# Products with the old RWKV and retention states moved between main products; rate transposes split over three places

## The reference

```python
# layer 0: FFN, RWKV-7 || retention, FFN;  layer 1: FFN, gated DeltaNet, FFN
def ab_mixer(h, ...):
    z = h @ ab_w_in                        # one projection for both head groups
    ...
    # RWKV-7, 8 heads, state S [64, 64]:
    sk = einsum('bhvk,bhk->bhv', S, kk_t)
    S = S * w_t - sk * (kk_t * a_t)^T + v_t * k_t^T
    o = einsum('bhvk,bhk->bhv', S, r_t)
    # retention, 4 heads, state S [128, 128]:
    o = inner + (q_c @ S) * xi
    S = g_chunk * S + kz_c^T @ v_c
    out = concat([gn(o_a) * gate, gn(o_b) * silu(gr)]) @ ab_w_out
def gdn_mixer(h, ...):
    ...                                    # conv, L2 norm, chunked gated delta rule
    g = -exp(A_log) * softplus(a_in + dt_bias)     # the decay rates
    beta = sigmoid(b_in)                           # the write rates
```

## Time and profile before

| what | value |
|---|---|
| median of three runs | 1469.47 us |
| the profiled execution's own time | 1475.2 us |
| its span in the trace | 1473.4 us |
| PE busy | 1409.7 us, 96% |
| DVE, ACT, POOL busy | 61%, 44%, 31% |
| mean granted TensorE clock | 0.986 of 2.4 GHz |

### The profile page before, as it was taken

How to read it: one execution, slowest core, us unless ns; L and a number is a source line. 1 busy time by engine, 2 the same in 40 slices (tenths; PEclk the granted TensorE clock), 3 DMA queues, 4 the chain that set the end, 5 groups by cost and what they waited for, 6 DMA issues and landing times.

```text
span 1473.4 us, 30676 instructions
## 1 busy us (share of the span) xinstructions
PE 1409.7 (96%) x12120; PEld 1341.9 (91%) x12120; DVE 902.7 (61%) x1204; ACT 648.0 (44%) x983; POOL 455.2 (31%) x464
## 2 busy tenths in 40 slices
PE   7999999887999999999999999999998899999996
PEld 7999999877979799999999999998987769999996
DVE  4444456976564465654577775568777466655544
ACT  4333336534234354333453443377683345333333
POOL 3333032632324122215211127431016651211343
PEclk9999999999998999999999999999998999999999
DMA  7555543311224155555445555434334015555541
GB/s 284 170 159 185 162 152 100 103 32 31 92 87 151 65 193 159 169 165 177 147 140 159 162 176 177 142 95 143 118 120 146 31 72 186 157 159 168 181 158 52
DMA packets 50623, 203.39 MB, mean 138 GB/s; under 512 B 5697, under 2 KB 5697, under 8 KB 49761
## 3 DMA queue, kind: packets, MB, share of 16 engines
q1 hardware_dynamic: 46224, 181.03, 38.6%
q0 software_dynamic: 4016, 19.81, 3.7%
q10 hardware_dynamic: 288, 1.18, 0.2%
HBM read 192.17 MB, written 9.83 MB: 137 GB/s over the span
## 4 chain that ended last, share of the span: by engine, by line
PE 84%; DVE 8%; ACT 4%; issue 3%; POOL 1%; DMA 0%; ACTq 0%; POOLq 0%; DVEq 0%
PE gemm L2634 23%; PE gemm L2638 23%; PE gemm L2635 23%; DVE wlo L2571 2%; ACT whi L2566 2%; PE gemm L2670 1%; PE job L1763 1%; PE job L876 1%; PE job L1702 0%; PE job L551 0%; PE job L2643 0%; PE job L1670 0%; POOL xsum L3177 0%; PE job L894 0%; DVE M L2296 0%
## 5 line engine op out<-in xcount | busy, mean ns | idle before, releaser
L2634 PE MATMUL gemm<-xhi,whi 128*128 128x290 f32 (+1 forms) x2032 | 615.4, 303 | 18.2 <-DVE wlo L2571 16.2
L2571 DVE TENSOR_TENSOR wlo<-raw,whi 128x1024 fp32r<-128x1024 f32 (+1 forms) x319 | 437.5, 1372 | 305.9 <-ACT whi L2566 303.4
L2566 ACT ACTIVATE whi<-raw 128x1024 fp32r<-128x1024 f32 (+1 forms) x319 | 358.4, 1123 | 599.3 <-PE gemm L2638 595.7
L2638 PE MATMUL gemm<-xlo,whi 128*128 128x290 f32 (+1 forms) x2032 | 606.9, 299 | 1.8 <-DVE xlo L407 1.5
L2635 PE MATMUL gemm<-xhi,wlo 128*128 128x290 f32 (+1 forms) x2032 | 604.0, 297 | 0.0
L2634 PEld LDWEIGHTS gemm<-xhi,whi 128*128 128x128 f32 x2032 | 386.6, 190 | 32.4 <-DVE wlo L2571 19.0
L2638 PEld LDWEIGHTS gemm<-xlo,whi 128*128 128x128 f32 x2032 | 385.8, 190 | 3.3 <-DVE xlo L407 2.0
L2635 PEld LDWEIGHTS gemm<-xhi,wlo 128*128 128x128 f32 x2032 | 386.6, 190 | 1.7
L2634 PE MATMUL gemm<-hhi,whi 128*128 128x288 f32 x704 | 209.6, 298 | 2.6 <-POOL hlo L3193 1.9
L2635 PE MATMUL gemm<-hhi,wlo 128*128 128x288 f32 x704 | 209.6, 298 | 0.0
L2638 PE MATMUL gemm<-hlo,whi 128*128 128x288 f32 x704 | 209.2, 297 | 0.0
(11 more groups left out here) (449 smaller groups left out, 1505.6 us busy)
## 6 DMA issues: line engine op xcount, KB each, us to landing
raw<-in_w_dram SPq DMA_DIRECT2D x255, 512.0 KB, 3.5
raw<-in_w_dram SPq DMA_DIRECT2D x64, 704.0 KB, 4.1
M<-in_ret_in_dram POOLq DMA_DIRECT2D x1, 2048.0 KB, 10.6
out_ret_s_dram<-M POOLq DMA_DIRECT2D x1, 2048.0 KB, 9.2
s_space<-in_gdn_in_dram POOLq DMA_DIRECT2D x4, 512.0 KB, 5.2
M<-in_gdn_in_dram POOLq DMA_DIRECT2D x4, 512.0 KB, 5.7
out_gdn_s_dram<-s_space POOLq DMA_DIRECT2D x4, 512.0 KB, 4.2
out_gdn_s_dram<-M POOLq DMA_DIRECT2D x4, 512.0 KB, 6.7
```

The costliest lines, as they stand in the source:

```text
L2566: nc.scalar.activation(whi[c % SPL][:, 0:w], raw[c % RAW][:, 0:w], ACT.Copy).then_inc(hi_ready, 1)
L2571: nc.vector.tensor_tensor(wlo[c % SPL][:, 0:w], raw[c % RAW][:, 0:w], whi[c % SPL][:, 0:w].bitcast(F32), ALU.subtract).then_inc(lo_ready, 1)
L2634: pe.matmul(bank[:, 0:w_], whi[s][:, w], hi[:, f0 + q, 0:w_], start=first, stop=False)
L2638: mm = pe.matmul(bank[:, 0:w_], whi[s][:, w], lo[:, f0 + q, 0:w_], start=False, stop=last)
```

## The change

The old-state products are taken out of the pieces between units and called by `stage` (and by `first_half`) after each single main product, through a new argument `within`. `within_unit(k, n)` says what follows main product n of unit k of `zb`: in unit 4 the sixteen pairs of head pairs 0 and 1, in unit 5 those of head pairs 2 and 3 after the first sixteen main products and the eight sample values after the last eight, in unit 15 the sixteen retention products of heads 0 and 1 after its seventh to twenty-second main product. Heads 2 and 3 stand after the first eight main products of the two first halves of `abo`. The pieces after units 4, 14 and 15 and the work after the stage are put in a new order on PE, ACT and DVE. In the DeltaNet layer the write rates' transposes go behind unit 14 of `qk`, the decay rates' stay behind the stage, and the samples' rates' go behind unit 0 of `v`.

```diff
-            def from_state(h):
-                bank = start(("rQ", h))
-                for b in range(DB):
...
+            def from_state(h, b):
+                bank = rbanks[h]
+                mm = pe.matmul(bank[:, 4 * b:4 * b + 4], b_s0[:, h, b, :], b_qx[:, h, SEQ + 4 * b:SEQ + 4 * b + 4],
+                               start=True, stop=True)
...
+            def state_in_half(h):
+                def between(n):
+                    if n < DB:
+                        from_state(h, n)
+                rbanks[h] = start(("rQ", h))
+                return between
...
-            def old_products(ts):
...
+            def old_product(t, b):
+                o, at = (t * DB + b) * 8, SEQ + DS * b
+                mms = [pe.matmul(pbanks[e][half(e), o:o + 8], a_s0[half(e), t, b, :],
+                                 kr[half(e), t, :, at:at + DS], start=True, stop=True) for e in range(2)]
...
+            def sample_values(h, bank):
+                mm = pe.matmul(bank[NROW, h * 64:(h + 1) * 64], s_at[:, h, 64:96],
+                               a_nat[NROW, 2, 0, h * 64:(h + 1) * 64], start=True, stop=True)
...
+            def within_unit(k, n):
+                if k == 4:
+                    if n == 0:
+                        pe.wait_ge(sem("rwkv_in"), 16)
+                    if n < 16:
+                        old_product(n // DB, n % DB)
+                elif k == 5:
+                    if n < 16:
+                        old_product(2 + n // DB, n % DB)
+                    else:
+                        if n == 16:
+                            rbanks["sMV"] = start(("sMV", 0))
+                        sample_values(n - 16, rbanks["sMV"])
+                elif k == 15:
+                    if n == 6:
+                        pe.wait_ge(sem("qx"), 1)
+                        pe.wait_ge(sem("ret_in"), 16)
+                        for h in range(2):
+                            rbanks[h] = start(("rQ", h))
+                    if 6 <= n < 22:
+                        from_state((n - 6) // DB, (n - 6) % DB)
...
-            stage("zb", 1, lambda k: next(piece))
-            from_state(3)
+            stage("zb", 1, lambda k: next(piece), within=within_unit)
+            first_half("abo", 2, 0, state_in_half(2))
+            ret_out(2)
+            ret_sum("rgm", 0)
+            ret_sum("rgm", 1)
+            first_half("abo", 2, 1, state_in_half(3))
             ret_out(3)
+            ret_sum("rgv", 0)
             ret_sum("rgm", 2)
             ret_sum("rgv", 1)
-            first_half("abo", 2, 0)
...
-            ret_square(1)
-            ret_ln(0)
-            state_part(3)
             act.wait_ge(sem("y_rwkv"), 1)
             for d in range(4):
                 high_part(d, a_gate[:, d, :])
+            state_part(0)
...
+                if k == 14:
+                    bank = start(("gtokb", 0))
...
             def l2_sums(k):
+                if k == 0:
+                    sample_rates()
...
                         pe.matmul(bank[:, 0:w_], whi[s][:, w], hi[:, f0 + q, 0:w_], start=first, stop=False)
+                        if within:
+                            within(4 * i + j, 3 * q)
```

More of the change, by code:

```diff
@@ L835, in between_units @@
                     fin(mm, ("rS", j))
[L836 to L839, removed]
+                yield
                 pe.wait_ge(*out(("ratt", 1)))
@@ L1092, in ab_scalar @@
                 high_part(d, a_gate[:, d, :])
+            state_part(0)
+            state_part(1)
+            ret_copy(0)
+            ret_copy(1)
+            state_part(2)
+            ret_copy(2)
+            ret_square(0)
+            ret_square(1)
+            state_part(3)
             ret_copy(3)
+            ret_ln(0)
             ret_square(2)
@@ L1632, in decays, with write_rates @@
                 fin(pe.matmul(bank[:, 0:T], sel[R32, h, :], rows_g, start=True, stop=True), ("dgb", h))
[L1634 to L1640, removed]
+            def write_rates(k):
+                decays(k)
+                if k == 14:
+                    bank = start(("gtokb", 0))
+                    for ck in range(4):
+                        for e in range(2):
+                            mm = pe.matmul(bank[half(e), ck:16:4], rows_b[:, ch_of(ck)], C("ident")[0:8, e:8:2],
+                                           start=True, stop=True)
+                    fin(mm, ("gtokb", 0))
+            stage("qk", 5, write_rates)
             bank = start(("gtok", 0))
@@ L1647, in gdn_tensor, with sample_rates @@
             fin(mm, ("gtok", 0))
[L1648 to L1656, removed]
+            def sample_rates():
+                pe.wait_ge(sem("rows4"), 3)
+                for key, ns, rows in ((("gtok4b", 0), (0,), slice(0, HC)), (("gtok4", 0), (1, 2), R32)):
+                    bank = start(key)
+                    for n in ns:
+                        for g in range(2):
+                            at = 2 * (n - ns[0]) + g
+                            mm = pe.matmul(bank[:, at:at + 1], q_rows[n][:, hs(g), :], C("ones", rows)[:, 0:1],
+                                           start=True, stop=True)
+                    fin(mm, key)
             def l2_sums(k):
+                if k == 0:
+                    sample_rates()
                 for t in (2 * k - 2, 2 * k - 1):
@@ L2164, in gdn_vector, with from_rows @@
                      key)
[L2165 to L2168, removed]
+            def from_rows(k):
+                if k == 1:
+                    for key, n0, n in ((("gtok4b", 0), 0, 1), (("gtok4", 0), 1, 2)):
+                        dve.wait_ge(*full(key))
+                        read(V.tensor_copy(q_tok[:, n0:n0 + n, :], jb(key, 2 * n).rearrange("p (n g) -> p n g", n=n)),
+                             key)
+                l2_max(k)
+            env["stage"]("v", conv(16, from_rows))
             l2_max(8)
```

77 lines of the change are left out of this document (31 added, 46 removed).

## The result

| | before | after |
|---|---|---|
| median of four runs each, one chip | 1469.16 us (1467.29 to 1469.93) | 1497.16 us (1493.71 to 1498.37) |
| ratio | | 1.0189, 95% interval 1.0172 to 1.0205 |
| profiled execution | 1475.2 us | 1493.71 us |

A forecast was written before the change was run, and what follows sets the result against it. PE, busy 96% of the span, and its clock were taken to bound the kernel. Units 4 to 6 +26.7, retention -2.3 and rates -0.8 sum to +23.6 us, giving 1493 on the 1469.5 median, range 1473 to 1502.

The forecast's parts named there:

- PE and its clock bound these stages: PE busy 96% of the span, so its instructions and clock are nearly the whole time.
- An insertion with change of form: Units 4 and 5: a singly placed pair adds 0.45 us, making 0.58 per main product; 0.96 at half clock.
- The clock falls in the middle of unit 4 and stays low into unit 6: Clock falls half way through unit 4's sixteen insertions, until main products follow each other again in unit 6.
- Units 4 to 6: RWKV's insertions: unit 4 +8.9, between units -2.5, unit 5 +17.3, unit 6 and its small groups +3.0; sum +26.7 us.
- Retention -2.3: Unit 15 and first halves of `abo`: one of two low-clock stretches gone, -3.3; new wait +1.0; range -6.7 to +4.
- The wait on ACT: Before the first half of `abo`, PE waits for ACT to drain head 0's job bank: +1.0 us, between 0 and 1.4.
- Rates -0.8: Rates' transposes in three places: two more changes of form +0.8 us, clock expected to hold -1.6 us.
- Rival 1: Clock holds in units 4 and 5 because PE never idles: +6.9 us, so 1476; chance 0.15.
- rivals 2 and 3: Weight loads hidden even where the form changes, about 1461, chance 0.09; loads half hidden, no change, 1467 to 1472, chance 0.04.
- Rival 4: As forecast, but the clock also stays low through retention's 32 insertions: 1499 us; chance 0.07.

The follow-up runs named there:

- RWKV's part alone: Only RWKV's old-state products and sample values moved as in the changed kernel, retention and rates left as before the change: 1490.59 us, ratio 1.0144.
- groups of eight: Changed kernel with RWKV's pairs in four groups of eight and the sample values as one group: 1476.54 us, ratio 1.0056; second run 1484.77 us.
- kernel with 128x128 forms: Changed kernel with each pair of 64x64 products made one product with 128x128 weights and the same 8 columns: 1490.48 us, ratio 1.0134.

## Why the prediction was right, and where not

The forecast was 1493 (range 1473 to 1502), the measured median 1497.16. The mechanism held where most of the time lies, in units 4 to 6; that the sum came so near is in part luck (see the base). Point by point:

- **PE and its clock bound these stages.** Right: PE's busy time grew with the span.
- **An insertion with change of form.** The term was 0.45 us and a period 0.58 at full clock, 0.96 at half; measured 0.54 and 0.85. The half-clock value leaned on a row that scales by 1.7. The insertion scaled by 1.5, from 0.41 to 0.61: the pair itself by 1.8 (0.12 to 0.21), the change of form by 1.4 (0.29 to 0.40).
- **The clock falls in the middle of unit 4 and stays low into unit 6.** Right in the first profile: it fell at 389.00, after nine of sixteen insertions, and came back at 423.1. In RWKV's part alone it fell at 384.80, after three. The cause given, weight loads and products of few columns in place of streaming, is borne out by the 128-column run, which has the same loads and changes of form and kept the clock there.
- **Units 4 to 6.** +26.7 us forecast, +21.3 measured: up to the start of unit 5 +4.5 (forecast 8.9 - 2.5 = 6.4), from there +16.8 (forecast 17.3 + 3.0 = 20.3). The mis-sized term is the period: unit 5 is 24 x 0.85 = 20.4 us instead of 23.0, 2.6 less; unit 4, with nine insertions at 0.54 and seven at 0.85, 1.5 less. Another 1.0 is unit 6 with the small groups ahead of it, where the clock came back half way.
- **Retention -2.3.** The size came near (-1.0 in the first profile) but the step failed. It read the two low stretches of the earlier trace rows as the price of the blocks, and one as gained. The later one is not: it is missing in the second profile of before. At equal low time the change's order is 2.1 us slower. The wait on ACT, +1.0 in the forecast, was 0.72; with ACT's order turned round it goes. A second wait was put at nothing ("their chain is as long as before") and took 0.78. The single products cost what they cost in their block, as said.
- **Rates -0.8.** Measured -0.8, for the wrong reason. The -1.6 of the clock came in two kernels whose rates were unchanged (-1.5 each); against those, the two more changes of form cost 0.7, which is the +0.8 of the other term.
- **The base.** The sum was set against a profiled execution 5.7 us above the median and carried over to the median. But that execution had all four stretches, and the terms took three of them as given back, 3.2 + 3.3 + 1.6 = 8.1 us. Against the second profile of before, whose 1468.3 us is near the median, the first profile of the changed kernel has 21.3 + 3.0 = +24.3 in units 4 to 6, -1.0 + 3.1 = +2.1 in retention and -0.8 + 1.5 = +0.7 in the rates. That is +27.1, where the medians differ by 28.0. (The two executions differ by 25.4: the one of before took 2.3 us more ahead of unit 3, where nothing was changed, and +0.6 lies elsewhere.) So the change has no part that gains. From this base the forecast would have been 23.6 + 8.1 = 31.7, too much mainly by the mis-sized period. One error hid most of the other, and that is luck.
- **What the 24.3 are.** An estimate from the prices above: the 40 insertions at full clock are 40 x (0.41 - 0.12) = +11.6. The rest, 12.7, is the low clock over 34.1 us, 0.37 per us. Rival 1 (clock holds, +6.9) is seen in no execution of the changed kernel, whose mean clock was 0.982 at most, where the kernel before had 0.986 and more; rivals 2 and 3 fall with the 0.54 us. Rival 4, the clock low in retention too, came true in the second profile (1500.82).
- **Two slips in the sums.** With 1.14 us a period the sum is +32.5, not +32.7; and rival 4's +6.2 leaves out the wait of 1.0. Neither changes the range.

What stays open is what decides whether a given execution loses the clock in groups of eight or in retention's halves: the same instructions did both. Open too is whether the stretch behind unit 14 belongs to the old order's block.

## What to carry to other kernels

Few-column products are cheapest in one block of one array form: placed singly between wide products each pays the change of form, and the mixture lost the clock here with PE busy all the way into the fall (384.08 to 389.00). Before a low-clock stretch is booked as the price of a piece of code, look at a second profile of the same kernel; here three of four such stretches were gone in it. If small work must be spread, spread it in groups (no grouping was faster than the old blocks), and judge it by many executions: the fastest of five (1469.5) and a later one on another chip (1484.8) were the same kernel.

## What the runs showed of the hardware

- A change of array form and back between float32 products cost 0.29 us a group at full clock and 0.40 at half; each 64x64 pair in a group cost 0.12 and 0.21 (groups of one, two, four and eight).
- Widening products from 8 to 128 columns lengthened an insertion by 0.15 us at full clock (0.54 to 0.69) and kept the clock at 1.00 over 27.9 us, where the 8-column ones lost it.
- The mixture of main products and single 128x128 products, at 0.36 us a period, kept the clock through unit 15 in the first profile of the changed kernel and lost it there in the second (485.10); in the kernel with 128x128 forms it lost it in unit 4 (389.80).
- A microsecond at half clock cost 0.37 to 0.46 us in these mixtures: 12.7 over 34.1 in units 4 to 6, 8.6 over 20.4 with groups of eight, 3.1 over 6.8 in retention.
